# Moving the moving operands of a float32r kernel by 32 bytes within the SBUF partition

## The chip, the cores and the metric

One core of one Trainium2 chip runs the whole program. The metric is the device time of one execution in microseconds, the median of three runs: 864.35 us for the kernel before (863.39, 864.35 and 866.3).

## The reference, cut to what matters

One decoder layer over a sequence of 512 tokens of width 1024, all in float32:

```
h = modulate(rms_norm(x, g1), shift, scale)
x = x + 0.5 * gate * (silu(h @ w_g) * (h @ w_u)) @ w_out        # D_FF = 2816
h = modulate(rms_norm(x, gmix), shift, scale)
x = x + gate * concat(pool_mixer(hA), gmlp_mixer(hB)) @ w_mix_out
h = modulate(rms_norm(x, g2), shift, scale)
x = x + 0.5 * gate * (silu(h @ w_g) * (h @ w_u)) @ w_out
y = rms_norm(x, gfin)
```

Here `[hA ; hB] = h @ w_mix_in`. The shifts, scales and gates come from one product of the condition c with `w_ada`. Nearly all arithmetic is in the two feed-forward blocks and the two mixer projections.

## The kernel before, in words

**Arithmetic.** The large products run in float32r, and each is made of three matmuls. An operand A is split into `A_hi`, its value rounded to float32r by ScalarE, and `A_lo`, the rest, made by VectorE. The product is `W_hi*A_hi + W_hi*A_lo + W_lo*A_hi` (`product`, L1670 to L1674, and the same three in `half_product`, L1845 to L1849). In a row of the profile such a matmul reads `ps<-moving,stationary`: the first name behind the arrow streams through the array, the second is loaded as weights by an LDWEIGHTS ahead of it.

**Tiling.** The activations stand transposed, features in the partitions and 512 tokens along the free dimension: 8 tiles of 128 features for `h_hi`, `h_lo`, `y_hi` and `y_lo`, 11 tiles at a time for the feed-forward product `b_hi`, `b_lo`. Three kinds of product are made from them:

- Plain products (`pair`, `plain`, `down2`): 512 columns a matmul. The down projections of both feed-forward blocks, the first tiles of their up projections and the mixer's projections are made so.
- Strassen products (`strassen`, `half_product`): the rest of the up projections, 34 items of seven half products. Each has four steps k and three matmuls a step, 256 columns a matmul. Their moving operands are halves of `h_hi` and `h_lo`, or sums of such halves in `sums_hi` and `sums_lo`; their weights stand in `sw_hi`, `sw_lo_a` and `sw_lo_b`.
- Half-width products (`pair_half`, `down2_half`): 256 columns a matmul, at the ends of the blocks, so that the norm of the first half of the tokens can begin early.

In one place the roles are turned: `v_tiles` (L1965 to L1974) streams weights through the array with `h_hi` and `h_lo` as the stationary operand. Its first half streams `v_split`, its second half `w_split`.

**Order of the work.** Each engine has a program written out by hand, tied to the others by semaphores. SP loads raw weights, ScalarE and VectorE split them one or two items ahead of TensorE, and TensorE goes from product to product. In the Strassen parts a matmul follows a weight load each time, with no wait between them but for the semaphores at an item's pieces.

**Placement in memory.** Nothing gives an address. The helper `sb` (L154) enters a tile in a scope, and the tiles of a scope stand one after the other, each rounded up to 32 bytes; when a scope is left, its space is given out again. So the order of the `sb` calls (L161 to L230) sets every address. Worked out in bytes within a partition, with what is left over by division by 128:

| tile | address | modulo 128 | role in the large products |
|---|---|---|---|
| `xT` | 16512 | 0 | none |
| `w_split` | 59520 | 0 | weights (moving in `v_tiles`, second half) |
| `sw_hi` | 61568 | 0 | weights |
| `sw_lo_b` | 75904 | 0 | weights |
| `h_hi`, `h_lo` | 106176, 122560 | 64 | moving (weights in `v_tiles`) |
| `sums_hi`, `sums_lo` | 138944, 155328 | 64 | moving |
| `y_hi`, `y_lo` | 138944, 155328 | 64 | moving |
| `v_split` | 155328 | 64 | moving in `v_tiles`, first half |
| `b_hi`, `b_lo` | 171712, 194240 | 64 | moving |
| `aside` | 216768 | 64 | unused, 64 bytes wide |
| `sw_lo_a` | 216832 | 0 | weights |

All strides inside these tiles are multiples of 512 bytes, so every matmul of a tile has its tile's remainder. `aside` is never read or written: it only brings `sw_lo_a` to a multiple of 128. `out_tok` and `vrow` begin at 106176 too, in scopes left before `h_hi` is placed. `ada_first`, `x_tok`, `v_raw`, `v_tok`, `xa`, `pooled`, `more_raw`, `xs` and others stand in scopes behind `h_lo`, and overlap the sums and the feed-forward product in space but not in time.

Of the kernel before, what the change touches and what calls it, by code (L numbers as in the profile page):

```python
# [24 lines left out]
P = 128  # L25
# [11 lines left out]
def build_program(nc, x, c, w_ada, b_ada, norm_ffn1_g, ffn1_w_in, ffn1_w_out, norm_mix_g, w_mix_in,  # L37
# [115 lines left out]
    with ctx:  # L153
        def sb(name, shape, dt=F32, scope=ctx):  # L154
            return scope.enter_context(nc.sbuf_tensor(name, shape, dt))
# [33 lines left out]
            vrow = sb("vrow", [P, P], F32, over_h)  # L189
        with ExitStack() as over_h:  # L190
            out_tok = sb("out_tok", [P, NT, D], F32, over_h)
        h_hi = sb("h_hi", [P, KD, T], F32R)
        h_lo = sb("h_lo", [P, KD, T], F32R)
        with ExitStack() as over_a:
# [31 lines left out]
        sums_lo = sb("sums_lo", [P, 4, KA, TH], F32R)  # L226
        b_hi = sb("b_hi", [P, GF, T], F32R)
        b_lo = sb("b_lo", [P, GF, T], F32R)
        aside = sb("aside", [P, 16])
        sw_lo_a = sb("sw_lo_a", [P, 5 * BL], F32R)  # L230


# [1905 lines left out]
```

How the kernel before makes its waits and increments, by code:

```python
            def raw_free(chunk):  # L416
                if not (isinstance(chunk, int) and chunk < 2):
                    sp.wait_ge(lo_ready, chunk - 1)
# [15 lines left out]
            def load_two(w, col, s, chunk):  # L435
                if chunk > MIXIN + 3:
                    raw_free(chunk)
                elif s:
                    sp.wait_ge(raw_full[1], (MIXIN + 1) // 2 * 32 + 32)
                for g in range(2):
                    sp.dma_start(pair_view(w_raw, s)[:, g], kpn(w)[:, :, col + g * P:col + (g + 1) * P])\
                      .then_inc(raw_full[s], 16)
# [11 lines left out]
            def load_ada(part):  # L455
                b = int(part in ADA_IN[1])
                n = ADA_IN[b].index(part)
                for s in range(2):
                    if n:
                        sp.wait_ge(ada_link, used(ADA_IN[b][n - 1], (s + 1) * KA // 2))
                    k0 = part % 2 * KA + s * KA // 2
                    sp.dma_start((ada_raw, more_raw)[b][:, s], w_ada_v[:, k0:k0 + KA // 2, ada_cols(part)])\
                      .then_inc(ada_full[b][s], 16)
# [31 lines left out]
            def host_free(f, i):  # L496
                if i - 2 in HOSTED[f]:
                    sp.wait_ge(ada_link, used(HOSTED[f][i - 2]))
# [1 line left out]
            def sw_free(f, i, whole=True):  # L501
                if i < 2:
                    sp.wait_ge(lo_ready, UP_AT[f] + PLAIN[f] - 1 + i)
                    if i:
                        sp.wait_ge(chunk_done, UP_AT[f] + PLAIN[f] - 1)
                else:
# [1160 lines left out]
        @block.tensor  # L1668
# [155 lines left out]
            pe.wait_ge(first_turned, KD)
```

## Time and profile before

| | |
|---|---|
| median of 3 runs | 864.35 us (863.39 to 866.3) |
| the profiled execution, its own time | 861.77 us |
| its span, first to last instruction | 860.0 us |
| mean granted clock of TensorE | 0.992 of 2.4 GHz |
| TensorE busy | 834.3 us, 97% |
| matmuls, weight loads | 5767, 5767 |

The span is what the trace covers; 1.8 us of the execution's own time lie around it. The duration that the profile gives a matmul runs from its start to its modelled end and overlaps the next one, so the pace of TensorE is read from the distance between starts and not from the duration. Of the names on a row, `L1847 ... ps<-sums_lo,sw_hi 128*128 128x256 f32 x544` means 544 matmuls of line 1847, with `sums_lo` moving in 256 columns and `sw_hi` stationary.

### The profile page before, as it was taken

What the parts mean: (1) busy time and instruction counts of PE and PEld (TensorE: products, weight loads), DVE (VectorE), ACT (ScalarE), POOL (GpSimd) and SP (SyncE); (2) the same over time, 40 slices, a digit from 0 to 9 for tenths busy, and PEclk for the clock granted to TensorE, in tenths of its full rate; (3) what the DMA queues carried; (4) which work ended last, traced back from release to release, by engine and by line L of the source; (5) the groups of instructions that cost most, each with busy time, mean ns of one, the idle gap of its engine ahead of it and who ended that gap; (6) DMA issues with size and microseconds to landing.
All of it is one profiled execution on the core that took longest, in us unless ns stands there. A gap on an engine that the chain in (4) does not pass through costs nothing.

```text
span 860.0 us, 14160 instructions
## 1 busy us (share of the span) xinstructions
PE 834.3 (97%) x5767; PEld 744.5 (87%) x5767; DVE 641.9 (75%) x919; ACT 381.2 (44%) x528; POOL 48.3 (6%) x56
## 2 busy tenths in 40 slices
PE   5999999999999999999999999899999999999996
PEld 4678889887999998887887899899988899999886
DVE  4469987876888878858657779988793588885443
ACT  6232436211666662333425256666611366665323
POOL 0000000000010000000430000000000000100000
PEclk8899999999999999999999999999999999999999
DMA  9998466776666765863433422587763568763222
GB/s 275 289 291 275 128 176 189 225 236 157 152 158 169 187 204 174 248 174 94 143 96 113 140 75 74 141 183 176 210 204 102 133 155 181 159 170 111 72 68 98
DMA packets 214781, 142.02 MB, mean 165 GB/s; under 512 B 6216, under 2 KB 193724, under 8 KB 214716
## 3 DMA queue, kind: packets, MB, share of 16 engines
q1 hardware_dynamic: 209764, 132.19, 53.0%
q0 software_dynamic: 4896, 8.92, 7.3%
q8 instruction: 45, 0.74, 0.4%
q14 instruction: 20, 0.16, 0.1%
q10 hardware_dynamic: 56, 0.01, 0.0%
HBM read 130.08 MB, written 2.10 MB: 154 GB/s over the span
## 4 chain that ended last, share of the span: by engine, by line
PE 88%; DVE 6%; ACT 2%; DMA 2%; issue 1%; SPq 0%; ACTq 0%; DVEq 0%
PE ps L1672 16%; PE ps L1674 15%; PE ps L1673 15%; PE ps L1845 12%; PE ps L1849 12%; PE ps L1847 12%; PE ps L1780 1%; DVE h_lo L1080 1%; PE ps L1971 1%; DVE xs L1073 1%; PE ps L1973 1%; PE ps L1972 1%; DMA sw_raw<-sw_raw 1%; DMA sw_raw<-in_ffn_w_in_dram 1%; DVE w_split L1039 1%
## 5 line engine op out<-in xcount | busy, mean ns | idle before, releaser
L1845 PE MATMUL ps<-sums_hi,sw_hi 128*128 128x256 f32 x544 | 150.3, 276 | 1.4 <-ACT ev L833 1.4
L1847 PE MATMUL ps<-sums_lo,sw_hi 128*128 128x256 f32 x544 | 150.2, 276 | 0.0
L1672 PE MATMUL ps<-b_hi,sw_hi 128*128 128x512 f32 (+1 forms) x374 | 143.8, 384 | 0.0
L1673 PE MATMUL ps<-b_lo,sw_hi 128*128 128x512 f32 (+1 forms) x374 | 140.7, 376 | 0.0
L801 ACT CAST sw_hi<-sw_raw 128x1024 fp32r<-128x1024 f32 (+2 forms) x102 | 119.8, 1180 | 31.2 <-DVE sw_raw L1254 22.8
L1845 PE MATMUL ps<-h_hi,sw_hi 128*128 128x256 f32 x408 | 112.8, 276 | 3.2 <-DVE sw_lo_a L1267 3.2
L1847 PE MATMUL ps<-h_lo,sw_hi 128*128 128x256 f32 x408 | 112.6, 276 | 0.0
L1849 PE MATMUL ps<-sums_hi,sw_lo_a 128*128 128x256 f32 x408 | 112.6, 276 | 0.0
L1845 PEld LDWEIGHTS ps<-sums_hi,sw_hi 128*128 128x128 f32 x544 | 102.1, 188 | 1.8 <-issue 1.3
L1847 PEld LDWEIGHTS ps<-sums_lo,sw_hi 128*128 128x128 f32 x544 | 102.1, 188 | 0.0
L1267 DVE TENSOR_TENSOR sw_lo_a<-sw_raw,sw_hi 128x1024 fp32r<-128x1024 f32 x68 | 99.0, 1455 | 3.1 <-ACT sw_hi L801 3.0
L1672 PE MATMUL ps<-h_hi,w_split 128*128 128x512 f32 (+1 forms) x240 | 92.8, 387 | 6.1 <-DVE h_lo L1080 5.8
L1674 PE MATMUL ps<-h_hi,w_split 128*128 128x512 f32 (+1 forms) x240 | 91.5, 381 | 0.0
L1673 PE MATMUL ps<-h_lo,w_split 128*128 128x512 f32 (+1 forms) x240 | 90.8, 378 | 0.0
L1673 PEld LDWEIGHTS ps<-b_lo,sw_hi 128*128 128x128 f32 x374 | 70.3, 188 | 13.5
L1672 PEld LDWEIGHTS ps<-b_hi,sw_hi 128*128 128x128 f32 x374 | 70.3, 188 | 12.4
L1845 PEld LDWEIGHTS ps<-h_hi,sw_hi 128*128 128x128 f32 x408 | 76.6, 188 | 3.9 <-issue 3.8
L1847 PEld LDWEIGHTS ps<-h_lo,sw_hi 128*128 128x128 f32 x408 | 76.6, 188 | 0.1
L1849 PEld LDWEIGHTS ps<-sums_hi,sw_lo_a 128*128 128x128 f32 x408 | 76.6, 188 | 0.0
L1849 PE MATMUL ps<-h_hi,sw_lo_a 128*128 128x256 f32 x272 | 75.1, 276 | 0.0
L826 ACT CAST sw_hi<-sw_raw 128x1408 fp32r<-128x1408 f32 (+1 forms) x32 | 40.3, 1261 | 73.9 <-PE ps L1674 67.3
L1674 PE MATMUL ps<-b_hi,sw_lo_b 128*128 128x512 f32 (+1 forms) x198 | 72.7, 367 | 0.0
(192 smaller groups left out, 1575.0 us busy)
## 6 DMA issues: line engine op xcount, KB each, us to landing
sw_raw<-in_ffn_w_in_dram SPq DMA_DIRECT2D x170, 256.0 KB, 4.4
sw_raw<-in_w_ada_dram SPq DMA_DIRECT2D x16, 1024.0 KB, 5.6
sw_raw<-in_ffn_w_out_dram SPq DMA_DIRECT2D x32, 384.0 KB, 4.7
sw_raw<-in_ffn_w_out_dram SPq DMA_DIRECT2D x32, 320.0 KB, 3.9
w_raw<-in_ffn_w_in_dram SPq DMA_DIRECT2D x19, 512.0 KB, 5.5
sw_raw<-sw_raw POOLq DMA_DIRECT2D x34, 256.0 KB, 3.8
ada_raw<-in_w_ada_dram SPq DMA_DIRECT2D x16, 512.0 KB, 5.5
ada_first<-in_w_ada_dram SPq DMA_DIRECT2D x14, 512.0 KB, 7.4
```

The lines of the kernel that those rows point to most:

```text
L801: nc.scalar.copy(sw_hi[:, j0 * BL:j1 * BL], sw_raw[:, i % 2, j0 * BL:j1 * BL])\
L826: nc.scalar.copy(down_hi(m)[:, c], sw_raw[:, i % 2, c]).then_inc(sw_hi_ready[f], 1)
L1039: ins = nc.vector.tensor_tensor(lo[:, c], raw[:, c], hi[:, c].bitcast(F32), ALU.subtract)
L1073: nc.vector.scalar_tensor_tensor(dst, src, gs[:, n, k:k + 1], r, ALU.mult, ALU.mult)\
L1080: nc.vector.scalar_tensor_tensor(h_lo[:, k, cols], xs[:, k, cols] if n != 1 else work[:, SCALED[i % 4], cols], mod_col(3 * n, k), h_hi[:, ...
L1267: nc.vector.tensor_tensor(lo_piece(c)[:, skip:], sw_raw[:, i % 2, j0 * BL + skip:j1 * BL], sw_hi[:, j0 * BL + skip:j1 * BL].bitcast(F32), ...
L1672: nc.tensor.matmul(dst, w_h, a_h, start=start, stop=False)
L1673: nc.tensor.matmul(dst, w_h, a_l, start=False, stop=False)
L1674: return nc.tensor.matmul(dst, w_l, a_h, start=False, stop=stop)
L1845: nc.tensor.matmul(dst, w_h[:, k, :], src_hi[:, k, :], start=start and k == 0, stop=False, skip_group_check=True)
L1847: nc.tensor.matmul(dst, w_h[:, k, :], src_lo[:, k, :], start=False, stop=False, skip_group_check=True)
L1849: ins = nc.tensor.matmul(dst, w_l[:, k, :], src_hi[:, k, :], start=False, stop=stop and k == KA - 1, skip_group_check=True)
```

## The change

A tile of 8 floats (32 bytes) a partition, `aside_h`, is placed ahead of `h_hi`, and `aside` shrinks from 16 floats to 8. All that stands between them moves up by 32 bytes: `h_hi`, `h_lo`, `y_hi`, `y_lo`, `sums_hi`, `sums_lo`, `b_hi`, `b_lo`, `v_split` and the other tiles of those scopes (`ada_first`, `c_wide`, `x_tok`, `v_raw`, `more_raw`, `xs`, `v_tok`, `pooled` among them). They stand at 96 modulo 128 then. `sw_lo_a` keeps its address, as do `w_split`, `sw_hi`, `sw_lo_b`, `out_tok`, `vrow` and all that is placed ahead of them. No instruction, wait or transfer is added, taken away or put in another order.

```
--- before.py
+++ after.py
@@ -189,6 +189,7 @@
             vrow = sb("vrow", [P, P], F32, over_h)
         with ExitStack() as over_h:
             out_tok = sb("out_tok", [P, NT, D], F32, over_h)
+        aside_h = sb("aside_h", [P, 8])
         h_hi = sb("h_hi", [P, KD, T], F32R)
         h_lo = sb("h_lo", [P, KD, T], F32R)
         with ExitStack() as over_a:
@@ -226,7 +227,7 @@
         sums_lo = sb("sums_lo", [P, 4, KA, TH], F32R)
         b_hi = sb("b_hi", [P, GF, T], F32R)
         b_lo = sb("b_lo", [P, GF, T], F32R)
-        aside = sb("aside", [P, 16])
+        aside = sb("aside", [P, 8])
         sw_lo_a = sb("sw_lo_a", [P, 5 * BL], F32R)
```

## Rows read from the trace of the kernel before

**Rows 1.** The page: span, busy time of each engine, granted clock.

```profile
span 860.0 us, 14160 instructions
...
PE 834.3 (97%) x5767; PEld 744.5 (87%) x5767; DVE 641.9 (75%) x919; ACT 381.2 (44%) x528; POOL 48.3 (6%) x56
...
PEclk8899999999999999999999999999999999999999
```

**Rows 2.** The page: the chain that ended last, by engine.

```profile
PE 88%; DVE 6%; ACT 2%; DMA 2%; issue 1%; SPq 0%; ACTq 0%; DVEq 0%
```

**Rows 3.** Groups of TensorE by line and shape: moving, stationary, count | busy us, mean ns.

```profile
L1847 PE MATMUL ps<-sums_lo,sw_hi 128*128 128x256 f32 x544 | 150.2, 276 | 0.0
...
L1673 PE MATMUL ps<-b_lo,sw_hi 128*128 128x512 f32 x330 | 128.4, 389 | 0.0
...
L1847 PE MATMUL ps<-h_lo,sw_hi 128*128 128x256 f32 x408 | 112.6, 276 | 0.0
...
L1673 PE MATMUL ps<-h_lo,w_split 128*128 128x512 f32 x208 | 81.9, 394 | 0.0
...
L1673 PE MATMUL ps<-y_lo,w_split 128*128 128x512 f32 x48 | 18.8, 391 | 0.0
...
L1673 PE MATMUL ps<-b_lo,sw_hi 128*128 128x256 f32 x44 | 12.3, 280 | 0.0
...
L1673 PE MATMUL ps<-y_lo,w_split 128*128 128x256 f32 x32 | 9.0, 280 | 0.0
...
L1673 PE MATMUL ps<-h_lo,w_split 128*128 128x256 f32 x32 | 8.9, 279 | 0.0
```

**Rows 4.** Timeline of TensorE, plain products: start us, us, instruction.

```profile
440.58 0.39 PE L1672 MATMUL ps<-h_hi,w_split 128*128 128x512 f32 x1
...
442.64 0.39 PE L1672 MATMUL ps<-h_hi,w_split 128*128 128x512 f32 x1
```

**Rows 5.** Timeline of TensorE, v projection, first half.

```profile
392.60 0.39 PE L1973 MATMUL ps<-v_split,h_lo 128*128 128x512 f32 x1
...
393.96 0.39 PE L1973 MATMUL ps<-v_split,h_lo 128*128 128x512 f32 x1
```

**Rows 6.** Timeline of TensorE, v projection, second half.

```profile
397.84 0.39 PE L1972 MATMUL ps<-w_split,h_hi 128*128 128x512 f32 x1
...
399.24 0.39 PE L1972 MATMUL ps<-w_split,h_hi 128*128 128x512 f32 x1
```

**Rows 7.** Timeline of TensorE, Strassen products.

```profile
299.73 0.28 PE L1845 MATMUL ps<-h_hi,sw_hi 128*128 128x256 f32 x1
...
300.86 0.28 PE L1847 MATMUL ps<-sums_lo,sw_hi 128*128 128x256 f32 x1
```

**Rows 8.** Timeline of TensorE, last down product, first its fast part, then its slow one.

```profile
848.32 0.28 PE L1672 MATMUL ps<-b_hi,sw_hi 128*128 128x256 f32 x1
...
849.34 0.28 PE L1672 MATMUL ps<-b_hi,sw_hi 128*128 128x256 f32 x1
...
850.70 0.28 PE L1672 MATMUL ps<-b_hi,sw_hi 128*128 128x256 f32 x1
...
852.12 0.28 PE L1672 MATMUL ps<-b_hi,sw_hi 128*128 128x256 f32 x1
```

**Rows 9.** Timeline of all engines around a matmul with no weight load behind it.

```profile
212.39 0.19 PEld L1674 LDWEIGHTS ps<-b_hi,sw_lo_b 128*128 128x128 f32 x1
...
212.61 0.40 PE L1674 MATMUL ps<-b_hi,sw_lo_b 128*128 128x512 f32 x1
...
214.26 0.19 PEld L1845 LDWEIGHTS ps<-h_hi,sw_hi 128*128 128x128 f32 x1 [1.68 <-issue]
```

**Rows 10.** Groups of VectorE that write tiles at either offset.

```profile
L1039 DVE TENSOR_TENSOR w_split<-w_raw,w_split 128x1024 fp32r<-128x1024 f32 x8 | 9.6, 1222 | 0.5 <-ACT w_split L693 0.4
...
L1230 DVE TENSOR_TENSOR sums_lo<-xs,sums_hi 128x1024 fp32r<-128x1024 f32 x6 | 7.3, 1219 | 0.0
```

More of the change, by code:

```diff
@@ L191, in build_program @@
             out_tok = sb("out_tok", [P, NT, D], F32, over_h)
+        aside_h = sb("aside_h", [P, 8])
         h_hi = sb("h_hi", [P, KD, T], F32R)
@@ L228, in build_program @@
         b_lo = sb("b_lo", [P, GF, T], F32R)
-        aside = sb("aside", [P, 16])
+        aside = sb("aside", [P, 8])
         sw_lo_a = sb("sw_lo_a", [P, 5 * BL], F32R)
```

## The prediction

> **What bounds the kernel now.** I read the busy times first. TensorE is busy for 834.3 of 860.0 us, and the granted clock stands at nine tenths or more from the third slice on [rows 1]; the chain that ended last is TensorE for 88% [rows 2]. So the time is the number of matmuls times their pace. No instruction is added or moved, and only the pace can change. Next come the counts. In each kind of product three lines issue equally many matmuls, so one line is read and taken three times [rows 3]. Plain products, 512 columns: 330 + 208 + 48 = 586, times 3 is 1758. Strassen products: 544 + 408 = 952, times 3 is 2856. Half-width products: 44 + 32 + 32 = 108, times 3 is 324. The v projection has 96 more (2 halves x 4 steps x 4 token tiles x 3), with the roles of weights and activations turned.
>
> Then the pace, from the distance between starts in the timeline, over a stretch of 6 to 12 matmuls without a break. The reader is to see that it depends on where the operands stand, and that it is not the 213.3 or 106.7 ns that 512 or 256 columns would take at 2.4 GHz.
>
> - Plain, moving at 64 modulo 128, weights at 0: 442.64 - 440.58 = 2.06 us for 9, or 228.9 ns [rows 4].
> - v projection, first half, moving at 64, stationary at 64: 1.36 us for 6, or 226.7 ns [rows 5].
> - v projection, second half, moving at 0, stationary at 64: 1.40 us for 6, or 233.3 ns [rows 6].
> - Strassen, moving at 64, weights at 0: 1.13 us for 10, or 113.0 ns [rows 7].
> - Half width, the same tiles in one product at two paces: 1.02 us for 9, or 113.3 ns, and after a break with other matmuls 1.42 us for 12, or 118.3 ns [rows 8].
>
> That is 402.4 + 10.9 + 11.2 + 322.7 + 38.3 = 785.5 us of TensorE's 834.3. The loss against the bare column count is not made by the weight load alone: the matmul at 212.61 has no load beside it (the next comes at 214.26) and still has 0.40 us, where its neighbours with loads have 0.39 [rows 4, 9]. It belongs to the reading of the moving operand, or to how one matmul follows the other.
>
> **The change, part by part.** All large products but the second half of the v projection get moving operands at 96. No row shows 96, so each pace is bounded from both sides by the rows at 64 and at 0. On a circle of 128, 96 lies halfway between them (128 is 0 again).
>
> *Plain products.* Lower end 226.7 ns, the fastest 512 columns of the trace [rows 5]: 2.2 ns less, times 1758 is 3.9 us gained. Upper end 233.3 ns, the moving operand at 0 [rows 6]: 4.4 ns more, 7.7 us lost. I take the middle between today's pace and the one at 0, 231.1 ns: 2.2 ns more, times 1758 is +3.9 us. Offset 64 with either partner is faster than offset 0, so a step from 64 towards 0 is likelier to cost than to gain.
>
> *Strassen products.* Lower end: today's 113.0 ns is the lowest pace at 256 columns in the trace, so nothing gained. Upper end 118.3 ns [rows 8]: 5.3 ns more, times 2856 is 15.1 us lost. I take no change. Both paces occur with the same tiles at the same addresses, so which of them holds depends on how a stretch begins, which the change leaves alone. Here each weight load fills the stretch of its matmul too, which is another steady pattern than that of the plain products.
>
> *Half-width products.* 5 ns less at best, times 324 is 1.6 us gained. I take no change; the worst is that of the Strassen products scaled, under 2 us.
>
> *v projection.* First half between 226.7 and 233.3 ns; the middle costs 3.3 ns x 48, +0.2 us. In the second half the stationary operand alone moves; I take nothing.
>
> *The other tiles that move*, one answer for all: VectorE's subtraction of 1024 columns takes 1222 ns into `w_split` at 0 and 1219 ns into `sums_lo` at 64 [rows 10], so it does not see such offsets. Transfers into `x_tok`, `ada_first`, `v_raw` and `more_raw` are the same in number and size and still begin at a multiple of 32 bytes. Both are covered by TensorE's stream; without that cover 3 ns an instruction is still nothing.
>
> *Sum.* +3.9 + 0.2 = +4.1 us. The profiled execution took 861.77 us (860.0 of span and 1.8 around it), which gives 865.9. That execution lies 2.6 us under the median of 864.35, and the same difference on the median gives 868.4. No stall goes away and none is added; TensorE is only a little slower, and everything that waits for it starts that much later.
>
> [...]
>
> **The rivals.**
>
> *No difference.* If what counts is on which half of a 128-byte stretch an operand begins, 96 is like 64: both lie in the upper half, and all paces stay. For it: the paces between 64 and 0 could be two classes with nothing between. Against it: nothing shows that 32 bytes are too fine to count. Time 864.35. The Trainium skill, SBUF — State Buffer, section "Who interferes with whom", says that TensorE never waits on anyone and has two independent read ports; by that rule too the placement of moving against stationary operands would not matter, and the trace agrees in so far as a lone matmul is no faster [rows 9].
>
> *The plain products reach the fastest pace.* Perhaps the distance between moving and stationary operand counts: 0 gives 226.7 ns, 64 gives 228.9, and the new distance of 96 is 32 on the circle, so the pace may fall too. Price: -3.9 us in the plain products, and -1.6 where half-width ones take their fast pace: 858.8. For it: the first half of the v projection. Against it: its second half has the distance 64 as well and is slowest, so distance alone does not order the rows.
>
> *The loss shrinks in all products.* Today's loss is 15.6 ns in 228.9 and 6.3 ns in 113.0; without it 27.4 + 18.0 = 45.4 us would go, down to 819. Nothing in the trace comes near it, as all placements lose at least 13 ns on 512 columns.
>
> *The Strassen products fall to the slow pace.* This ends well on the slow side: at 96 each item would run at 118.3 ns, as the last down product does in its second part, for +15.1 us beside the +4.1: 883.5. It decides from the first item at 124 us on, and half of them slipping is already +7.5 us. For it: the slow pace exists, and today's 113.0 leaves no room below. Against it: nearly all Strassen items find the fast pace today, from whatever beginning.
>
> **How the numbers follow.** About 0.3%, or 2.6 us, is what a measurement of this kernel can tell from no change; that is 1.5 ns on each plain matmul or 0.9 ns on each Strassen matmul. Chances: my forecast of slightly slower 0.28, no difference 0.26, the fastest pace for the plain products 0.27, a smaller loss in all products 0.05, Strassen at the slow pace in whole or in part 0.14. So slower is 0.42, same 0.26 and faster 0.32. The predicted time is that of the first case, 868.4. Cases of both signs hold most of the chance: the forecast's own range is 867 (just over the bound of 0.3%) to 872.3 (the plain products at 233.3 ns: 7.7 + 0.2 more than today). The range for 8 in 10 goes from 857.5, a little under the fastest pace with the scatter of the runs, to 883.5; the smaller loss in all products and anything beyond the slow pace are left out.
>
> **What would show each step right or wrong.** In the timeline of the changed kernel: the distance of starts in plain products at 440 us (231 ns if I am right, 226.7 for the faster rival, 228.9 for none), in the Strassen products at 300 us (113.0 or 118.3), in both halves of the v projection (the second unchanged at 233.3), and in half-width products. Instruction counts, VectorE's and ScalarE's means and the waits should stay as they are. I am wrong if the plain pace does not rise, if the Strassen pace moves at all, or if TensorE's sum of paces stays and the time changes elsewhere.

## The result, and the profile after

The changed kernel takes 886.63 us (median of 4 runs, 885.48 to 890.44) against 865.33 us for the kernel before in the same series (4 runs, 863.39 to 868.41): a ratio of 1.0238 [1.0189, 1.0287]. It is slower by some 21 us, on the side that I forecast, but five times as much as I forecast and 3 us beyond the upper end of the range. The profiled execution took 885.79 us.

The page of the changed kernel, the lines that answer to [rows 1, 2], and two rows of its groups. Line numbers are one higher than before, since the change adds a line at 192.

```profile
span 884.1 us, 14160 instructions
...
PE 859.0 (97%) x5767; PEld 763.8 (86%) x5767; DVE 641.6 (73%) x919; ACT 379.7 (43%) x528; POOL 48.2 (5%) x56
...
PEclk9999999999999999999999999999999999999999
...
PE 88%; DVE 5%; SPq 2%; DMA 2%; ACT 1%; issue 1%; DVEq 0%; ACTq 0%
...
L1848 PE MATMUL ps<-sums_lo,sw_hi 128*128 128x256 f32 x544 | 155.1, 285 | 0.0
...
L1674 PE MATMUL ps<-b_lo,sw_hi 128*128 128x512 f32 (+1 forms) x374 | 142.8, 382 | 0.0
```

The instructions are the same in number, the clock is no lower, and VectorE is busy for 641.6 us as before. The span is 24.1 us longer and TensorE's busy time 24.7 us. So nothing new waits: the matmuls themselves follow each other more slowly. The waits of TensorE that the profile lists add up to 19.5 us against 20.0 before. The two largest inside the large products (what it waited for: us in total, times, longest) are those of before, where `h_lo` cost 5.8 us and `sw_lo_a` 3.2:

```profile
PE ps L1673 <- DVE h_lo L1081: 5.6, 5, 3.1
...
PE ps L1846 <- DVE sw_lo_a L1268: 3.0, 2, 1.9
```

The timeline of TensorE in the changed kernel (start us, us, instruction), first and last matmul of four stretches. The first answers to [rows 7] and holds 84 distances, as many as an item has matmuls; the others answer to [rows 4, 5, 6] and hold 18 each.

```profile
289.72 0.29 PE L1850 MATMUL ps<-sums_hi,sw_lo_b 128*128 128x256 f32 x1
...
299.83 0.29 PE L1850 MATMUL ps<-sums_hi,sw_lo_b 128*128 128x256 f32 x1
...
440.60 0.40 PE L1675 MATMUL ps<-h_hi,w_split 128*128 128x512 f32 x1
...
444.80 0.40 PE L1675 MATMUL ps<-h_hi,w_split 128*128 128x512 f32 x1
...
403.41 0.39 PE L1974 MATMUL ps<-v_split,h_lo 128*128 128x512 f32 x1
...
407.49 0.39 PE L1974 MATMUL ps<-v_split,h_lo 128*128 128x512 f32 x1
...
407.72 0.40 PE L1972 MATMUL ps<-w_split,h_hi 128*128 128x512 f32 x1
...
411.93 0.40 PE L1972 MATMUL ps<-w_split,h_hi 128*128 128x512 f32 x1
```

Strassen: 10.11 us / 84 = 120.4 ns, where it was 113.0. Plain: 4.20 / 18 = 233.3, where it was 228.9. First half of the v projection: 4.08 / 18 = 226.7, as before, though its moving operand now stands at 96 too. Second half: 4.21 / 18 = 233.9, where it was 233.3.

One item is a small sample, so from here on a **pace** is the mean distance between the starts of neighbouring matmuls of one kind over a whole trace, pauses left out (distances over 160 ns at 256 columns and over 300 ns at 512). Before: Strassen 113.4, plain 229.3, half width 117.5. After: 120.0, 233.3 and 119.7. The distances summed, pauses included: Strassen products from 327.9 to 346.0 us (+18.1), plain from 407.2 to 414.0 (+6.8), half width from 40.2 to 40.8 (+0.6), v projection from 22.6 to 21.9 (-0.7). That is +24.8 us against +24.1 of span. Three quarters of the loss are in the term that I had put at nothing.

### The profile page after: what moved, and what is told of

Read it like the earlier page. It is cut to its first block, busy times and chain, and to the rows that moved or that the text cites. A ratio compares the mean times of both kernels' runs of the same rounds, so it can differ in the third digit from the quotient of the medians.

```text
span 884.1 us, 14160 instructions
## 1 busy us (share of the span) xinstructions
PE 859.0 (97%) x5767; PEld 763.8 (86%) x5767; DVE 641.6 (73%) x919; ACT 379.7 (43%) x528; POOL 48.2 (5%) x56
## 4 chain that ended last, share of the span: by engine, by line
PE 88%; DVE 5%; SPq 2%; DMA 2%; ACT 1%; issue 1%; DVEq 0%; ACTq 0%
PE ps L1673 15%; PE ps L1675 15%; PE ps L1674 15%; PE ps L1848 13%; PE ps L1850 13%; PE ps L1846 12%; PE ps L1972 1%; PE ps L1974 1%; DMA ada_first<-in_w_ada_dram 1%; PE ps L1973 1%; SPq L471 1%; DVE h_lo L1081 1%; DMA sw_raw<-in_ffn_w_in_dram 1%; DVE xs L1074 1%; PE ps L1781 1%
## 5 line engine op out<-in xcount | busy, mean ns | idle before, releaser
L1848 PE MATMUL ps<-sums_lo,sw_hi 128*128 128x256 f32 x544 | 155.1, 285 | 0.0
L1846 PE MATMUL ps<-sums_hi,sw_hi 128*128 128x256 f32 x544 | 153.4, 282 | 0.3 <-ACT ev L834 0.3
L1674 PE MATMUL ps<-b_lo,sw_hi 128*128 128x512 f32 (+1 forms) x374 | 142.8, 382 | 0.0
L802 ACT CAST sw_hi<-sw_raw 128x1024 fp32r<-128x1024 f32 (+2 forms) x102 | 119.7, 1179 | 35.2 <-DVE sw_raw L1255 23.9
L1846 PE MATMUL ps<-h_hi,sw_hi 128*128 128x256 f32 x408 | 114.7, 281 | 3.0 <-DVE sw_lo_a L1268 3.0
L1850 PE MATMUL ps<-sums_hi,sw_lo_a 128*128 128x256 f32 x408 | 116.4, 285 | 0.0
L1848 PE MATMUL ps<-h_lo,sw_hi 128*128 128x256 f32 x408 | 115.7, 284 | 0.0
L1850 PE MATMUL ps<-h_hi,sw_lo_a 128*128 128x256 f32 x272 | 77.2, 284 | 0.0
```

What stands on the lines that cost most here:

```text
L802: nc.scalar.copy(sw_hi[:, j0 * BL:j1 * BL], sw_raw[:, i % 2, j0 * BL:j1 * BL])\
L1674: nc.tensor.matmul(dst, w_h, a_l, start=False, stop=False)
L1846: nc.tensor.matmul(dst, w_h[:, k, :], src_hi[:, k, :], start=start and k == 0, stop=False, skip_group_check=True)
L1848: nc.tensor.matmul(dst, w_h[:, k, :], src_lo[:, k, :], start=False, stop=False, skip_group_check=True)
L1850: ins = nc.tensor.matmul(dst, w_l[:, k, :], src_hi[:, k, :], start=False, stop=stop and k == KA - 1, skip_group_check=True)
```

## The experiments

All of them change addresses alone. A difference of 8 floats is 32 bytes. **Distance** is the address of the moving operand less that of the weights, modulo 128 where nothing else is said: 64 before, 96 after. Each time is beside runs of the kernel before on the same chip. A table of the paces stands behind the first two groups.

### Whose address counts?

**d0_moving_at_0**: the moving operands at 0, weights at 0.

```
+        aside_h = sb("aside_h", [P, 16])
...
-        aside = sb("aside", [P, 16])
```

> Moving operands and weights both at 0 modulo 128. Distance theory (the pace depends on moving minus stationary offset, as the first half of the v projection kept 226.7 ns with both at 96): plain products at 226.7 ns, so about 4 us less there than before; Strassen products at 113.3 ns or slower, unknown; if they keep it, about 861 us. Own-address theory (an operand is slow by where the moving one stands, as in the second half of the v projection, moving at 0): plain products at 233.3 ns, Strassen slower too, 873 us or more.

Measured: 880.73 us against 863.83, ratio 1.0203 [1.0175, 1.0231]. Strassen at 118.8, plain at 232.8.

**d32_moving_at_32**: the moving operands at 32 (`aside_h` of 24 floats, `aside` of 24).

> Moving operands at 32, weights at 0. Distance theory: 32 is as far from 0 as 96 on a circle of 128; if only the distance counts, plain products near 233 ns, Strassen near 120 ns, the time like the changed kernel, about 886 us; if the sign counts, anything between 861 and 886. Own-address theory (an operand that does not begin at a multiple of 64 is slow): 886 us too.

Measured: 881.51, ratio 1.0217 [1.0182, 1.0252]. Strassen 117.7, plain 234.2. So every other offset tried with the weights at 0 is slower than 64.

**all_up_32**: moving operands at 96 as in the change, and all weights at 32, so that the distance is 64 as before.

```
+        aside_x = sb("aside_x", [P, 8])
         xT = ...
```

> All tiles 32 bytes up: moving operands at 96 as in the changed kernel, weights at 32, so the distance is 64 as before. Distance theory: the time of before, 865 us, plain products at 228.9 ns and Strassen at 113.3 ns. Own-address theory: the time of the changed kernel, 886 us, 233 and 120 ns.

Measured: 864.35 (10 runs) against 863.83 (13 runs), ratio 0.9996 [0.9959, 1.0032]; Strassen 113.6, plain 229.4. The offset of 96 is harmless in itself.

**weights_at_96**: moving operands left at 64, weights at 96; no operand stands where the change puts it.

```
+        aside_w = sb("aside_w", [P, 24])
...
+        aside_h = sb("aside_h", [P, 8])
...
-        aside = sb("aside", [P, 16])
+        aside = sb("aside", [P, 8])
```

In other words, all_up_32 is the kernel before moved up as a whole by 32 bytes, and weights_at_96 the changed kernel moved up as a whole by 96: every distance between two tiles of the large products is kept, modulo 256 too.

> Moving operands at 64 as before, weights at 96: moving minus weights is 96 modulo 128, the distance of the changed kernel, and no moving operand has another remainder than before. Distance theory: about 886 us, 233 and 120 ns. Own-address theory of the moving operand: 865 us. If the weights' own address counts, slower than before by an amount of its own.

Measured: 886.94, ratio 1.0275 [1.0245, 1.0304]; Strassen 120.0, plain 233.4, half width 119.7: the paces of the changed kernel, at a distance of -32 modulo 128, which is 96. As many matmuls from the same time on, in the timeline of this run, take the same 10.11 us:

```profile
289.75 0.28 PE L1847 MATMUL ps<-sums_hi,sw_hi 128*128 128x256 f32 x1
...
299.86 0.28 PE L1847 MATMUL ps<-sums_hi,sw_hi 128*128 128x256 f32 x1
```

These two runs settle the cause: the same moving address with the old distance loses nothing, and the new distance with the old moving address loses all of it.

### How the pace depends on the distance

**d0_modulo_256** and **d0_modulo_512**: `aside_h` of 48 and 112 floats, `aside` taken out, so that the distance is 0 modulo 256, and in the second run 0 modulo 512 as well.

> Moving operands at 128 modulo 256, as w_split, sw_hi, sw_lo_b and sw_lo_a are: the distance is 0 modulo 256, where the kernel with the moving operands at 0 had 0 modulo 128 but mostly 128 modulo 256. In the first half of the v projection the distance is 0 modulo 256 in every kernel so far, and its pace is 226.7 ns in every one. If bit 7 of the distance counts: plain products at 226.7 ns (4 us less than before), Strassen at 113.3 ns or less, 860 us. If only the distance modulo 128 counts: 880.7 us as with d0_moving_at_0, plain 232.8 and Strassen 118.8 ns, and the v projection is fast for another reason.

> The same with the distance 0 modulo 512 for all pairs. If bit 8 counts beside bit 7, this one and not the last is fast (860 us); if neither counts, both are at 880.7 us.

Measured: 877.79, ratio 1.0168 [1.0134, 1.0201], and 876.98, ratio 1.0162 [1.013, 1.0194], with the same paces: plain 227.1, the fastest of the study, and Strassen 120.0, as slow as at 96. Plain products of the first run, 18 distances:

```profile
449.76 0.39 PE L1672 MATMUL ps<-h_hi,w_split 128*128 128x512 f32 x1
...
453.85 0.39 PE L1672 MATMUL ps<-h_hi,w_split 128*128 128x512 f32 x1
```

4.09 / 18 = 227.2 ns, close to the 226.7 that I had read in [rows 5], where moving and stationary operand also have the distance 0. Against d0_moving_at_0, whose tiles were 128 apart modulo 256, the plain pace is 5.7 ns lower: 128 bytes do count.

The second half of the v projection confirms this. Its distance is modulo 256 not that of the plain products before, 64, but 192: `w_split` at 128 less `h_hi` at 192. The same run brings it to 0 (18 distances):

```profile
403.99 0.39 PE L1971 MATMUL ps<-w_split,h_hi 128*128 128x512 f32 x1
...
408.07 0.39 PE L1971 MATMUL ps<-w_split,h_hi 128*128 128x512 f32 x1
```

4.08 / 18 = 226.7 ns, where it was 233.3. Wherever a run gave it a distance modulo 256 that plain products had in another run, the paces are alike: 226.7 and 227.1 ns at 0, 233.6 and 233.3 at 96, 233.3 and 232.8 at 128, 234.2 and 234.2 at 160 (v projection in d0_modulo_256, d32_moving_at_32, d0_moving_at_0 and the changed kernel, plain products in d0_modulo_256, the changed kernel, d0_moving_at_0 and d32_moving_at_32).

**d80** and **d48**: distances in steps of 16 bytes, by a lead of 4 floats inside each moving tile.

> Moving operands at 80 modulo 128, weights at 0, by an unused lead of 16 bytes in each moving tile. Distance theory with a smooth course between 64 (863.8 us) and 96 (886.9 us): about 875 us. If the distance counts in steps of 32 bytes or coarser: 863.8 us as at 64. If 64 is a point of its own and all others are slow: 880 us or more.

> Moving operands at 48 modulo 128, weights at 0. Smooth course between 32 (881.5 us) and 64 (863.8 us): about 872 us. Steps of 32 bytes: 881.5 us as at 32. 64 a point of its own: 880 us or more.

Measured: 876.27, ratio 1.0157 [1.0119, 1.0195], and 875.41, ratio 1.0145 [1.0113, 1.0176].

The third column is the distance of the `hi` tiles from `w_split` and `sw_hi` modulo 256. The fourth says whether `sw_lo_a`, which the pads move as well, stands on the other half of 256 bytes than `sw_hi`; this turns out to matter further down.

| run | distance | modulo 256 | `sw_lo_a` on the other half | Strassen ns | plain ns | half width ns | ratio |
|---|---|---|---|---|---|---|---|
| before | 64 | 64 | yes | 113.4 | 229.3 | 117.5 | 1 |
| all_up_32 | 64 | 64 | yes | 113.6 | 229.4 | 116.5 | 0.9996 |
| d48 | 48 | 176 (`lo` tiles 48) | no | 117.8 | 231.1 | 117.6 | 1.0145 |
| d80 | 80 | 80 (`lo` tiles 208) | yes | 117.8 | 231.2 | 118.0 | 1.0157 |
| d0_modulo_256 | 0 | 0 | no | 120.0 | 227.1 | 119.5 | 1.0168 |
| d0_moving_at_0 | 0 | 128 | yes | 118.8 | 232.8 | 119.1 | 1.0203 |
| d32_moving_at_32 | 32 | 160 | no | 117.7 | 234.2 | 118.0 | 1.0217 |
| after | 96 | 96 | yes | 120.0 | 233.3 | 119.7 | 1.0238 |
| weights_at_96 | 96 | 96 | yes | 120.0 | 233.4 | 119.7 | 1.0275 |

Of the distances tried, plain products are fastest at 0 modulo 256 and next fastest at 64; Strassen products are fastest at 64. The two kinds want different placements. What 16 bytes alone cost is not shown: the lead makes each moving tile 128 bytes longer, so that in d48 and d80 the `lo` tiles stand on the other half of 256 bytes than the `hi` tiles, and d48 and d32_moving_at_32 moved `sw_lo_a` too. The rows that differ from before in the distance between moving operands and weights alone are the changed kernel, weights_at_96 and d0_moving_at_0.

### One part of the change at a time

**strassen_at_96**: distance 96 between the Strassen operands, 64 in the plain products (`h`, `y`, sums at 96, `w_split` at 32, `b` at 64). **plain_at_96**: the reverse (`w_split` at 96, `b` at 96).

> Only the Strassen products get the distance of the changed kernel, 96 (their sums and h at 96, their weights at 0); w_split stands at 32 and the feed-forward product at 64, so all plain and half-width products keep the distance 64. Distance theory: Strassen at 120.0 ns as in the changed kernel against 113.4 before, 6.6 ns x 2856 = 18.9 us more, 882.5 us, plain products at 229 ns. If the loss were in the plain products after all: 864 to 868 us.

> The other part alone: w_split at 96 under h and y at 64, and the feed-forward product at 96 over weights at 0, so all plain and half-width products have the distance 96 or 96 modulo 128, and all Strassen products keep 64. Distance theory: plain at 233.3 ns against 229.0, 4.3 x 1758 = 7.6 us more, half width at 119.7 against 117.6, 0.7 us, together 872 us, Strassen at 113.4 ns. The two parts add up to the changed kernel.

Measured: strassen_at_96 880.27, ratio 1.0169 [1.013, 1.0209], Strassen 119.4, plain 229.1 (up and mixer products) to 230.8 (down products, at their distance of before; no run explains this 1.4 ns), half width 116.2 to 117.4. plain_at_96 877.25, ratio 1.0117 [1.0078, 1.0157]; its profiled execution took 871.8, with plain at 233.3, and Strassen at 113.4 in three stretches but 118.6 in the fourth, from 686 us on. The excess ratios, 0.0169 and 0.0117, make 0.0286 together, as against 0.0238 for the change; the surplus of 0.0048 is no more than the intervals allow, and it would fit the Strassen stretches that fell to a slower pace in plain_at_96, which the change to the plain products was not to touch.

**best_of_both**: 0 modulo 256 in all plain products, 64 in the Strassen ones (`w_split` 64 bytes up, `b` 192 bytes up). It should have beaten both kernels.

> Each kind of product at its fastest distance: plain at 0 modulo 256 (w_split to 64 under h and y at 64, the feed-forward product to 0 over weights at 0), Strassen at 64 as before. Plain at 226.9 ns against 229.0: 2.1 x 1758 = 3.7 us less; second half of the v projection 226.7 against 233.3: 0.3 us less; half width 119.6 against 117.6: 0.6 us more. Together 3.4 us less than before, 860.2 us against 863.6, with Strassen at 113.4 ns. If the phase in which the products follow one another matters more than the distance, Strassen falls to 117 ns or slower and the time is above before.

Measured: 868.86 (12 runs), ratio 1.0043 [1.0018, 1.0068]. Plain came to 227.1 as planned, but Strassen ran at 117.8 in three of its four stretches, at a distance of 64 throughout. So 64 does not secure the fast pace.

### Two paces at one distance

**before_again_1, before_again_2, best_again**: the kernel before twice and best_of_both once, one profiled execution each, for what stays and what changes between executions.

> The kernel before, profiled once more. If a stretch's pace is fixed by the addresses and what precedes it: all four Strassen stretches at 113.4 ns, 861 to 863 us. If each execution falls into a pace at the start of a stretch: where this execution is slower than the first profile (861.77 us), a stretch at 117.7 ns makes up the difference (up to 4.3 ns x 924 = 4.0 us for each long stretch).

> The same once more: the same paces as in the other two profiles if they are fixed by the program, others if each execution chooses.

> best_of_both once more. Fixed by the program: its second stretch (216 to 320 us) at 113.4 ns and the other three at 117.7 ns again, 868 us. Chosen by each execution: another pattern, between 860.5 us (all fast) and 872.5 us (all slow), with plain products at 227.1 ns in any case.

Measured: 861.17, 865.95 and 872.0. The same program from the same time on in before_again_1, then in before_again_2 (84 distances each):

```profile
289.77 0.28 PE L1845 MATMUL ps<-h_hi,sw_hi 128*128 128x256 f32 x1
...
299.29 0.28 PE L1845 MATMUL ps<-h_hi,sw_hi 128*128 128x256 f32 x1
```

```profile
289.77 0.28 PE L1849 MATMUL ps<-h_hi,sw_lo_a 128*128 128x256 f32 x1
...
299.74 0.28 PE L1849 MATMUL ps<-h_hi,sw_lo_a 128*128 128x256 f32 x1
```

9.52 / 84 = 113.3 ns and 9.97 / 84 = 118.7 ns. In the second execution the stretch from 214 to 324 us, 924 matmuls, had a mean of 118.4, and the others 113.4: 5.0 ns x 924 = 4.6 us, against 4.8 us between the two spans (859.4 and 864.2). The first 23 matmuls of that stretch still ran at 113.3; then TensorE waited 1.2 us, and the other 900 or so ran at 118.6. In the profiles at this distance a run of matmuls keeps its pace until the next pause. All stretches at the slow pace would cost some 14 us (2856 x 5.0 ns), so this is enough to make the times of the kernel before scatter from 860 to 871 us; only three executions of it were profiled. best_again had 117.8 in all stretches.

Two paces are not peculiar to the distance 64. In the changed kernel the long runs of matmuls were at 120.2 to 120.6 ns, but from 560 to 636 us, behind a pause of 0.6 us, at 118.4 (84 distances, 118.3 ns):

```profile
579.77 0.28 PE L1846 MATMUL ps<-sums_hi,sw_hi 128*128 128x256 f32 x1
...
589.71 0.28 PE L1846 MATMUL ps<-sums_hi,sw_hi 128*128 128x256 f32 x1
```

**aligned_but_last**: as best_of_both, but the products just ahead of each Strassen stretch keep 64, on the idea that they decide how it begins.

```
+        far = (UP1 + PLAIN[0] - 1, UP2 - 1, UP2, UP2 + 1)
+        def w_parts(number):
+            at = [(2 * (number % 2) + q) * (FULL + 64) + (0 if number in far else 16) for q in range(2)]
...
+            at = m % 2 * D1_AT - (16 if m == KD - 1 else 0)
```

> Moving operands of every plain product at distance 0 (modulo 256) from their weights, except the products just ahead of a Strassen stretch, which keep the distance 64; all Strassen products and half-width passes keep 64. If the Strassen pace of a stretch is set by the distance of the products ahead of it, all stretches entered that way stay at 113.4 ns and about 1600 of the 1758 plain products take 227.1 instead of 229.0: 3 to 4 us less than before, 860.5. If a Strassen stretch can fall into the 117.7 pace for another reason (anything earlier in the program that differs), stretches of 924 or 756 matmuls show 117.7 to 118.4 and the time is 864 to 869, as with the variant that aligned all plain products.

Measured: 868.92, ratio 1.0054 [1.0026, 1.0082]. Plain 227.2, Strassen at 117.7, but for one item at 534 us at 113.3, which went over to 117.7 at the pause of 546 us. The idea falls.

What these layouts share is the place of `sw_lo_a`. `sw_hi` and `sw_lo_b` stand at 128 modulo 256. Before, `sw_lo_a` stands at 0; in best_of_both and aligned_but_last it had moved to 128, as a by-product of the new lengths. **lo_a_other_half** moves it alone, in the kernel before:

```
-        aside = sb("aside", [P, 16])
+        aside = sb("aside", [P, 48])
```

> The kernel before with sw_lo_a alone 128 bytes further up, so that all weights of a Strassen product have the same remainder modulo 256 (128), where before sw_lo_a stood at 0 and the others at 128. All distances modulo 128 stay at 64. Theory A (the fast Strassen pace needs the weights of the third matmul on the other half of 256 bytes than those of the first two): Strassen goes from 113.4 to 117.7 ns in most stretches, the time from 864 to between 868 and 876, plain products stay at 229. Theory B (which pace holds is decided by what precedes a stretch, or by chance): paces stay at 113.4 as in the kernel before, 864 within its scatter.

Measured: 872.51 (9 runs), ratio 1.0087 [1.0056, 1.0119]. Plain stays at 229.0 and Strassen is at 117.8 in all stretches, but for 11 matmuls between two hitches at 571 and 573 us, which ran at 113.3. In its timeline, from the same time on:

```profile
289.73 0.28 PE L1845 MATMUL ps<-sums_hi,sw_hi 128*128 128x256 f32 x1
...
299.62 0.28 PE L1845 MATMUL ps<-sums_hi,sw_hi 128*128 128x256 f32 x1
```

9.89 / 84 = 117.7 ns; 4.4 ns x 2856 is 12.6 us, and the span is 11.7 us longer than that of before_again_1. One tile moved by 128 bytes, with every distance modulo 128 unchanged, costs over a third as much as the change (0.0087 against 0.0238). Modulo 256 the move also takes the distance of the third matmul's operands from 192 to 64, so whether the half shared by the weights counts, or this distance, no run separates.

**aligned_lo_a_kept** is best_of_both with `sw_lo_a` back at 0 modulo 256; **lo_a_kept_again** is the same kernel once more: the profiled execution of the first took 1197.16 us at a granted clock of 0.654, is not in the ratio and shows no paces.

```
+        aside = sb("aside", [P, 32])
         sw_lo_a = sb("sw_lo_a", [P, 5 * BL], F32R)
...
-            return sw_lo_b[:, 0:DN] if m % 2 else sw_lo_a[:, 0:DN]
+            return sw_lo_b[:, 0:DN] if m % 2 else sw_lo_a[:, 32:32 + DN]
```

> The variant with all plain products at distance 0 modulo 256 (best_of_both), with sw_lo_a back at 0 modulo 256; the even down products read it 128 bytes further in, so that their distance stays 0 too. Theory A: Strassen back at 113.4 ns in all stretches, plain at 227.1, 864 less 3.8 us is 860.5, faster than both kernels. Theory B: Strassen at 117.7 in most stretches as before in this variant, 868 to 872.

> The same kernel as in the run before, whose profiled execution had a granted clock of 0.654 and showed no paces. Theory A: plain 227.1, Strassen 113.4 ns in all stretches, near 862. Since its timed executions spread from 862.4 to 875, I expect one to three of the four Strassen stretches at 117.7 instead, each worth 1.1 to 4 us.

Measured: ratio 1.0033 [0.9997, 1.007], its other 11 runs from 862.39 to 875.1 with a median of 868.65, where 860.5 was expected; the later execution 863.67, beside 861.65 for the kernel before. Its timeline, one item in the second and one in the fourth stretch:

```profile
289.80 0.28 PE L1847 MATMUL ps<-sums_hi,sw_hi 128*128 128x256 f32 x1
...
299.32 0.28 PE L1847 MATMUL ps<-sums_hi,sw_hi 128*128 128x256 f32 x1
...
729.81 0.28 PE L1849 MATMUL ps<-h_lo,sw_hi 128*128 128x256 f32 x1
...
739.77 0.28 PE L1849 MATMUL ps<-h_lo,sw_hi 128*128 128x256 f32 x1
```

113.3 ns and 118.6 ns. With `sw_lo_a` back, three of four stretches are fast again in this one profile, against one and none in the two profiles of best_of_both. The plain products have 227.1 to 227.4 ns and save their 3.9 us, and the slow fourth stretch gives back 5.2 ns x 924 = 4.8 us.

The times do not bear out the profile. With plain at 227.1 and Strassen at 113.4 the median would be near 860.5; at 868.65 more than half of the Strassen matmuls of this layout must run slow, if nothing else does. Five of its 11 runs are under 867 us, against one of 12 of best_of_both, and the two ratios, 1.0033 and 1.0043, are not told apart. So the half of `sw_lo_a` is shown to matter in the kernel before (lo_a_other_half), and not in this layout.

I count five long entries into the Strassen pace in each profiled execution: four stretches, the third of which has a pause behind its first item. Left out are the 23 matmuls ahead of a further pause at the start of the second stretch and behind that pause of the third, which go their own way (5 of 10 clear ones are fast with `sw_lo_a` on the other half). With `sw_lo_a` on the other half of 256 bytes than `sw_hi` (before, its two repetitions, all_up_32, plain_at_96, lo_a_kept_again) 26 of 30 entries were fast. With both on the same half (best_of_both, best_again, aligned_but_last, lo_a_other_half) 2 of 20 were. The slow pace differs too: 118.6 ns in the four slow entries of the first group, 117.8 in those of the second. These entries are few, and five of them come from a layout whose other runs were mostly slow, so the counts are no odds. What decides a single entry stays open. No layout of this study beats the kernel before.

## Why the prediction was wrong

- **What bounds the kernel, and the counts** (1758 plain, 2856 Strassen, 324 half width): right. With them the measured paces give the whole difference.
- **The variable.** The first step that failed is "On a circle of 128, 96 lies halfway between them", which bounded each pace by the moving operand's own offset. all_up_32 and weights_at_96 show that the distance to the weights counts, and the circle is one of 256 bytes: plain products took 227.1 ns at 0 and 232.8 at 128. I had the distance as a rival and gave it up because the second half of the v projection "has the distance 64 as well" and is slowest [rows 6]. That objection was wrong. Its moving operand stands 64 bytes behind the stationary one, which modulo 256 is 192 and not the 64 of the plain products; at 0, 96, 128 and 160 its pace is that of plain products at the same distance, within 0.5 ns. No other product ran wholly at 192, so the 233.3 ns of that row have nothing beside them.
- **Strassen, put at nothing with 15.1 us as the worst**: it cost 6.6 ns a matmul, 18.1 us by the sum of distances. This is the mis-sized term, and nearly all of the miss: 18.1 of some 21 us beyond the forecast. My reason was that both paces "occur with the same tiles at the same addresses, so which of them holds depends on how a stretch begins, which the change leaves alone". The premise was right and before_again_2 shows it; the conclusion was not. The placement decides whether the fast pace is to be had at all: at 96 no stretch came under 118.4 ns, and the mean of 120.0 lies above the upper bound of 118.3 [rows 8], which was the slow pace of another placement and so no bound.
- **Plain, +2.2 ns within -2.2 to +4.4**: +4.0 ns, 6.8 us instead of 3.9. The upper bound held.
- **v projection**: the first half stayed at 226.7 and did not go to 230, since both its operands moved and their distance is still 0. The second half, where I took nothing, rose by 0.9 ns (233.3 to 234.2 over the whole half). Neither shows in the sum.
- **Half width, nothing with 2 us at worst**: +2.2 ns, 0.6 us. **VectorE, ScalarE, transfers**: nothing, right (641.6 against 641.9 us).
- **The lone matmul** [rows 9]: 0.40 us beside 0.39 compares durations whose end is modelled, so it does not show that the weight load has no part in the loss.
- **The rivals.** "Strassen at the slow pace", 883.5 us at a chance of 0.14, was the mechanism; it fell short by 1.7 ns a matmul. "The plain products reach the fastest pace" exists, but at 0 modulo 256, the opposite direction from 96.
- **Pages and measurement.** The traces show 227.1 to 234.2 ns for 512 columns and 113.4 to 120.0 for 256 by placement alone. The Trainium skill, TensorE: Matmul & The Clock Gate, section "Back-to-back issue gap", gives spacings by column count without a word on addresses: about 216 ns at 512 by its formula for an isolated matmul, and about 131 ns measured for a stream of loads and matmuls. No stream of this case comes near the second, and the measurement decides that the placement counts. The Trainium skill, SBUF — State Buffer, section "Who interferes with whom", gives TensorE two read ports, one for the moving operand and one for the weight load, and calls them independent. That the pace depends on where the two operands stand to each other (weights_at_96, all_up_32) does not fit full independence; no run here shows which part of the chip makes the dependence.

## What to carry to other kernels

In a float32r kernel that TensorE bounds, treat the distance between the moving operand and the weights, modulo 256, as a parameter to be measured for each kind of product: here the 512-column products want 0 and the Strassen products of 256 columns want 64, and a wrong choice costs 1 to 2.8%. When any tile's length changes, print all addresses modulo 256, since a by-product of 128 bytes on one weight tile cost 0.9%. And read the pace in several stretches and executions before bounding it: one stretch at a slower pace shows that a second pace exists, not what it is at another placement.

## What was unexpected of the hardware

- The pace of float32r matmuls depends on moving less stationary address: plain from 227.1 (0 modulo 256) to 234.2 ns (160 modulo 256), Strassen from 113.4 (64) to 120.0 (96, and 0 modulo 256). A move of all operands together by 32 bytes changes nothing (all_up_32, 0.9996), and the turned roles of the v projection give the same paces at the same distance modulo 256.
- At distance 64 modulo 128 a back-to-back stream of 256 columns has two paces, 113.3 and 117.8 to 118.6 ns, and keeps one of them for up to 924 matmuls, until a pause; at 96 there are two as well, 118.4 and 120.2 to 120.6. Identical executions choose differently (861.17 and 865.95 us).
- In the kernel before, bringing the weights of all three matmuls of a step onto the same half of 256 bytes slows the Strassen products by 4.4 ns (lo_a_other_half, 1.0087). Over all layouts at 64, 2 of 20 long entries were fast where they stand so, and 26 of 30 where `sw_lo_a` stands on the other half, but aligned_lo_a_kept, where it does, was no faster over 11 runs than best_of_both, where it does not (1.0033 and 1.0043).
